# Linear attention rounds of a two-block model: heads innermost on TensorE, one masked copy per level over four score banks, the second exponents between two rounds, and no clearing of the score tile

## The reference, cut to what matters

```python
def step(state, inp):
    qc, kc, vc, gc = inp
    g = jnp.cumsum(gc, axis=2)
    seg = jnp.exp(jnp.where(tri[:, :, None], g[:, :, :, None, :] - g[:, :, None, :, :], -jnp.inf))
    att = jnp.sum(qc[:, :, :, None, :] * kc[:, :, None, :, :] * seg, axis=-1)
    o = (jnp.einsum('bhij,bhjv->bhiv', att, vc)
         + jnp.einsum('bhid,bhdv->bhiv', qc * jnp.exp(g), state))
```

## Time and profile before

| What | Value |
|---|---|
| median of 3 runs | 2586.05 us (2585.83 to 2586.1) |
| profiled execution, first to last instruction (its span) | 2580.6 us |
| the profiled execution's own time | not listed apart from its span; the median is 5.45 us above the span |
| mean granted TensorE clock | 0.968 of full speed |
| TensorE matmul busy | 2439.7 us (95%) |
| VectorE busy | 1693.0 us (66%) |
| ScalarE busy | 1374.6 us (53%) |
| GpSimd busy | 410.1 us (16%) |

### The profile page before, as it was taken

The page is one execution under the profiler, slowest core; times in us unless marked ns, Lnnn a source line. Parts: engine busy times, 40 slices in busy tenths (PEclk is TensorE's granted clock), DMA queues, the critical chain, the costliest instruction groups (busy, mean ns, idle before and its releaser), DMA issues.

```text
span 2580.6 us, 32016 instructions
## 1 busy us (share of the span) xinstructions
PE 2439.7 (95%) x11845; PEld 1981.6 (77%) x11845; DVE 1693.0 (66%) x2386; ACT 1374.6 (53%) x1737; POOL 410.1 (16%) x225
## 2 busy tenths in 40 slices
PE   7999899989988899999999999979989988998998
PEld 6987688888766687787787787868768877776886
DVE  4846565467564689898898898854555555355554
ACT  4543254445432578787787787735434434543443
POOL 2155000002540000000000000046510005550000
PEclk9998899989998899999999999989999998999999
DMA  7434375435331899999999999853465525346550
GB/s 222 169 109 147 100 260 195 133 100 186 130 132 34 289 346 366 331 341 353 331 357 336 331 364 329 284 161 129 170 225 202 183 89 170 128 150 212 196 196 33
DMA packets 381701, 549.38 MB, mean 213 GB/s; under 512 B 27221, under 2 KB 283593, under 8 KB 381465
## 3 DMA queue, kind: packets, MB, share of 16 engines
q1 hardware_dynamic: 377392, 535.82, 61.1%
q0 software_dynamic: 3920, 11.58, 1.7%
q10 hardware_dynamic: 288, 0.59, 0.1%
HBM read 546.91 MB, written 1.05 MB: 212 GB/s over the span
## 4 chain that ended last, share of the span: by engine, by line
PE 64%; DVE 3%; DMA 1%; ACT 1%; issue 1%; POOL 0%; DVEq 0%; ACTq 0%
PE mb L904 13%; PE mb L906 12%; PE mb L905 12%; PE pb L904 5%; PE pb L905 5%; PE pb L906 5%; PE pb L1349 2%; PE mb L1259 1%; PE pb L1299 1%; PE pb L887 1%; PE mb L1275 1%; DMA ring<-in_w_in 1%; PE mb L1385 0%; PE pb L1335 0%; PE pb L1334 0%
## 5 line engine op out<-in xcount | busy, mean ns | idle before, releaser
L2540 DVE TENSOR_TENSOR w_lo<-ring,w_hi 128x1024 fp32r<-128x1024 f32 x444 | 533.4, 1223 | 210.0 <-ACT w_hi L1645 184.2
L904 PE MATMUL mb<-w_hi,hT_hi 128*128 128x512 f32 x1232 | 493.5, 401 | 2.9 <-DVE w_lo L2540 2.6
L1645 ACT ACTIVATE w_hi<-ring 128x1024 fp32r<-128x1024 f32 x340 | 347.9, 1053 | 269.5 <-DMA ring<-in_w_in 101.9
L906 PE MATMUL mb<-w_lo,hT_hi 128*128 128x512 f32 x1232 | 481.0, 390 | 0.0
L756 POOL TENSOR_TENSOR w_lo<-ring,w_hi 128x1024 fp32r<-128x1024 f32 x152 | 373.3, 2484 | 457.1 <-ACT w_hi L1645 456.9
L904 PE MATMUL pb<-w_hi,hT_hi 128*128 128x512 f32 (+1 forms) x928 | 357.1, 385 | 10.2 <-DVE low_rows L2540 5.7
L2540 DVE TENSOR_TENSOR w_lo<-down_w,w_hi 128x1024 fp32r<-128x1024 f32 x242 | 293.6, 1223 | 87.6 <-ACT w_hi L1645 79.3
L905 PE MATMUL pb<-w_hi,low_rows 128*128 128x512 f32 (+1 forms) x928 | 347.6, 375 | 0.0
L906 PE MATMUL pb<-w_lo,hT_hi 128*128 128x512 f32 (+1 forms) x928 | 347.0, 374 | 0.0
L1794 ACT ACTIVATE w_hi<-ring 128x1024 fp32r<-128x1024 f32 x256 | 267.0, 1056 | 19.9 <-PE mb L906 13.0
L905 PE MATMUL mb<-w_hi,xg_lo 128*128 128x512 f32 x704 | 274.6, 390 | 0.0
(11 more groups left out here) (454 smaller groups left out, 3778.1 us busy)
## 6 DMA issues: line engine op xcount, KB each, us to landing
ring<-in_moe_w SPq DMA_DIRECT2D x128, 1024.0 KB, 7.9
ring<-in_w_in SPq DMA_DIRECT2D x50, 2048.0 KB, 8.1
down_w<-in_moe_w SPq DMA_DIRECT2D x88, 1024.0 KB, 11.3
third_gu<-in_moe_w SPq DMA_DIRECT2D x48, 1024.0 KB, 9.6
down_w<-in_w_ffn_down SPq DMA_DIRECT2D x22, 1024.0 KB, 10.0
ring<-in_w_out SPq DMA_DIRECT2D x8, 2048.0 KB, 8.0
ring<-in_ffn_w SPq DMA_DIRECT2D x16, 1024.0 KB, 7.9
ring<-in_w_ffn_gate SPq DMA_DIRECT2D x16, 1024.0 KB, 5.4
```

The source lines that it names most:

```text
L904: mm(o, a_hi, hi, start=start, stop=False)
L906: return mm(o, a_hi, lo, start=False, stop=stop)
L1645: f(w_hi[:, m % NPIECE], src, ACT.Copy).then_inc(w_hi_ready, 1)
L2540: return tt(dst, src, hi.bitcast(F32), ALU.subtract)
```

## The change

Five edits. (1) The four banks mb0 to mb3 are declared as one PSUM tensor of four banks, so that one instruction can read all four. (2) A helper `score_pairs` takes the heads of the retention and of the mLSTM in pairs: the wide product of both, then the narrow product of both. (3) In the rounds of the gated linear attention the loop over heads becomes the innermost. (4) `gla_put_levels` copies each level with one `copy_predicated` over all four banks (two per round in place of eight), and the last round with one copy in place of four; the clearing of probs is gone. (5) `gla_levels` is cut in two: `gla_exponents` and `gla_factors`; the second exponents are now made between the copies of round 0 and round 1, the second factors stay behind the copies of round 1, and the wait for round 1's products stands just ahead of the factors.

```diff
--- before.py
+++ after.py
@@ -416,7 +416,8 @@
         lat_s, lat_m, lat_r = small[:, 120:126], small[:, 126:130], small[:, 130:134]
 
         pb = [ctx.enter_context(nc.psum_tensor(f"pb{n}", [P, 512], F32)) for n in range(4)]
-        mb = [ctx.enter_context(nc.psum_tensor(f"mb{n}", [P, 512], F32)) for n in range(4)]
+        mb_all = ctx.enter_context(nc.psum_tensor("mb", [P, 4, 512], F32))
+        mb = [mb_all[:, n] for n in range(4)]
 
 
         filled, act_emptied, dve_emptied = sem("pb_filled"), sem("pb_act_emptied"), sem("pb_dve_emptied")
@@ -1030,6 +1031,19 @@
                 mm(bank[:, 0:S], kT[:, 0:P], qT, start=True, stop=True)
                 return mm(bank[:, S:S + P], kT[:, P:S], qT[:, P:S], start=True, stop=True)
 
+            def score_pairs(kT, qT):
+
+
+                for a in (0, 2):
+                    rows_of = lambda h: slice(64 * (h % 2), 64 * (h % 2) + 64)
+                    for h in (a, a + 1):
+                        r = rows_of(h)
+                        mm(mb[h][:, 0:S], kT[r, h // 2, 0:P], qT[r, h // 2, :], start=True, stop=True)
+                    for h in (a, a + 1):
+                        r = rows_of(h)
+                        ins = mm(mb[h][:, S:S + P], kT[r, h // 2, P:S], qT[r, h // 2, P:S], start=True, stop=True)
+                return ins
+
             def weigh_values(banks, v, w=64):
                 for i in range(T):
                     for h in range(NH):
@@ -1105,10 +1119,7 @@
                 gate(L, 1, 0, 1)
                 pe.wait_ge(ml_arg, 4 * (L + 1))
                 pe.wait_ge(conv_ready, 2 * L + 2)
-                for h in range(NH):
-                    r = 64 * (h % 2)
-                    ins = score_head(mb[h], conv[r:r + 64, 8 + h // 2, :], conv[r:r + 64, 6 + h // 2, :])
-                ins.then_inc(scores_mm, 1)
+                score_pairs(conv[:, 8:10], conv[:, 6:8]).then_inc(scores_mm, 1)
                 gate(L, 1, 1, 0)
                 pe.wait_ge(probs_ready, 3 * L + 2)
                 weigh_values(mb[0:2], lambda j, h: u_ml[:, j, h * (ML_V + 1):(h + 1) * (ML_V + 1)], ML_V + 1)
@@ -1124,10 +1135,7 @@
                 merge(L, 0)
                 pe.wait_ge(qkt_ready, L + 1)
                 pe.wait_ge(o_read, 4 * L + 2)
-                for h in range(NH):
-                    r = 64 * (h % 2)
-                    ins = score_head(mb[h], ret_qk[r:r + 64, 2 + h // 2, :], ret_qk[r:r + 64, h // 2, :])
-                ins.then_inc(scores_mm, 1)
+                score_pairs(ret_qk[:, 2:4], ret_qk[:, 0:2]).then_inc(scores_mm, 1)
                 gate(L, 2, 0, 0)
                 gate(L, 2, 0, 1)
                 pe.wait_ge(probs_ready, 3 * L + 3)
@@ -1143,20 +1151,17 @@
                         pe.wait_ge(gla_kq, 2 * L + rnd // 2 + 1)
                     if rnd:
                         pe.wait_ge(gla_put, 5 * L + rnd)
-                    for h in range(NH):
-                        r = slice(32 * h, 32 * h + 32)
-                        if rnd < 4:
-                            for s_ in range(2):
-                                lev = 2 * rnd + s_
-                                for i in range(T):
-                                    t_ = slice(i * P, (i + 1) * P)
-                                    kk, qq = (gla_k[r, lev % 4, t_], gla_q[r, lev % 4, t_]) if lev < 7 else (
-                                        ch_in[r, 11, t_], ch_in[r, 10, t_])
-                                    ins = mm(mb[h][:, s_ * S + i * P:s_ * S + (i + 1) * P], kk, qq, start=True, stop=True,
-                                             tile_position=(32 * h, 0))
-                        else:
-                            ins = mm(mb[h][:, 0:P], gla_k[r, 3, 0:P], gla_q[r, 3, P:S], start=True, stop=True,
-                                     tile_position=(32 * h, 0))
+                    for n in range(2 * T if rnd < 4 else 1):
+                        lev, t_ = 2 * rnd + n // T, slice(n % T * P, (n % T + 1) * P)
+                        for h in range(NH):
+                            r = slice(32 * h, 32 * h + 32)
+                            if rnd == 4:
+                                kk, qq = gla_k[r, 3, 0:P], gla_q[r, 3, P:S]
+                            elif lev < 7:
+                                kk, qq = gla_k[r, lev % 4, t_], gla_q[r, lev % 4, t_]
+                            else:
+                                kk, qq = ch_in[r, 11, t_], ch_in[r, 10, t_]
+                            ins = mm(mb[h][:, n * P:(n + 1) * P], kk, qq, start=True, stop=True, tile_position=(32 * h, 0))
                     ins.then_inc(gla_mm, 1)
                     if rnd < 2:
                         gate(L, 3, 0, rnd)
@@ -2113,11 +2118,9 @@
                             else:
                                 link(ins)
 
-            def gla_levels(L, half):
-
-
-                if half:
-                    v.wait_ge(gla_mm, 5 * L + 2)
+            def gla_exponents(L, half):
+
+
                 for n in range(4):
                     b = 1 << (4 * half + n)
                     g = gT[:].rearrange("p (m s b) -> p m s b", s=2, b=b)
@@ -2126,23 +2129,27 @@
                     tt(e[:, :, 0], ref, g[:, :, 0], ALU.subtract)
                     ins = tt(e[:, :, 1], g[:, :, 1], ref, ALU.subtract)
                 ins.then_inc(gla_arg, 1)
+
+            def gla_factors(L, half):
+
                 v.wait_ge(gla_exp, 2 * L + half + 1)
+                if half:
+                    v.wait_ge(gla_mm, 5 * L + 2)
                 tt(gla_k, gla_e, ch_in[:, 11:12].to_broadcast([P, 4, S]), ALU.mult)
                 tt(gla_q, gla_e, ch_in[:, 10:11].to_broadcast([P, 4, S]), ALU.mult).then_inc(gla_kq, 1)
 
             def gla_put_levels(L, rnd):
 
                 v.wait_ge(gla_mm, 5 * L + rnd + 1)
-                for h in range(NH):
-                    if rnd == 4:
-                        ins = cp(probs[:, h, P:S], mb[h][:, 0:P])
-                        continue
-                    dst = probs[:, h, :].rearrange("p (a i) -> p a i", i=P)[:, 0:3:2, :]
+                if rnd == 4:
+                    ins = cp(probs[:, :, P:S], mb_all[:, :, 0:P])
+                else:
+                    dst = probs[:].rearrange("p h (a i) -> p h a i", i=P)[:, :, 0:3:2, :]
                     for s_ in range(2):
-                        src = mb[h][:, s_ * S:(s_ + 1) * S].rearrange("p (a i) -> p a i", i=P)
-                        msk = levmask[:, 2 * rnd + s_].bitcast(U32).unsqueeze(1).to_broadcast([P, T, P])
+                        src = mb_all[:, :, s_ * S:(s_ + 1) * S].rearrange("p h (a i) -> p h a i", i=P)
+                        msk = levmask[:, 2 * rnd + s_].bitcast(U32).unsqueeze(1).unsqueeze(1).to_broadcast([P, NH, T, P])
                         ins = nc.vector.copy_predicated(dst, msk, src)
-                        if not (h == NH - 1 and s_ == 1):
+                        if s_ == 0:
                             link(ins)
                 ins.then_inc(gla_put, 1)
                 v.wait_ge(gla_put, 5 * L + rnd + 1)
@@ -2279,7 +2286,8 @@
                     tt(probs[:, h, 0:S], mb[h][:, 0:S], retdecay[:, h, 0:S], ALU.mult)
                     ins = tt(probs[:, h, S:384], mb[h][:, S:384], retdecay[:, h, 0:P], ALU.mult)
                 ins.then_inc(probs_ready, 1)
-                gla_levels(L, 0)
+                gla_exponents(L, 0)
+                gla_factors(L, 0)
                 take_y(L, 2)
                 for i in range(T):
                     ins = cp(y[:, i], mb[i][:, 0:MW])
@@ -2289,10 +2297,10 @@
                 merge(L, 1)
 
                 v.wait_ge(pv_mm, 4 * L + 3)
-                link(nc.vector.memset(probs[:].rearrange("p h n -> p (h n)"), 0.0))
                 gla_put_levels(L, 0)
+                gla_exponents(L, 1)
                 gla_put_levels(L, 1)
-                gla_levels(L, 1)
+                gla_factors(L, 1)
                 gla_put_levels(L, 2)
                 merge(L, 2, (0,))
                 gla_put_levels(L, 3)
```

## The result

The changed kernel takes 2566.48 us (median of 4 runs, 2562.36 to 2568.26) against 2586.07 us before (4 runs): a ratio of 0.9932, 95% interval 0.9914 to 0.995. That is 19.6 us faster, 3.5 us above the predicted 2563 and inside the range.

What follows compares the result with a forecast made beforehand. Bound: a chain hopping between TensorE and VectorE from round 0 to the weighing. Gains 13.1 (layer 0) + 10.7 (layer 1) + 0.4 (score pairs) - 1.0 (clock) = 23.2 us, so 2586.05 becomes 2563 us; range 2556 to 2573.

Steps and rivals of the forecast that it cites:

- rival (a): Before round 2, GpSimd goes first and both second factors wait: 2.2 us more per layer, 2567.5 us; chance 0.22.
- my own case: First factor ahead of GpSimd, second waits for one low part, round 2 at 242.75: 2563 us; chance 0.40.
- Rounds 1.10 us: On TensorE, heads innermost bring round start to next gate from 2.75 to 1.10 us, saving 1.65 per round.
- rival (c): New head order does nothing, or a wide masked copy costs four narrow ones: 2571 us; chance 0.18.
- Masked copy 1.26 us: On VectorE, a masked copy of 1024 elements takes 1260 ns, two in a chain some 2.55 us.
- Round 1 and exponents: In layer 0, round 1 starts at 233.9 in place of 236.55; the moved exponents end at X = 235.65.
- Both arrive at X + 2.6: First factor and GpSimd's low part due together after the exponents' end X; second factor done at about X + 7.1.
- 14.3 us from round 2 to the weighing: VectorE's chain there takes 14.3 us in place of 20.27 in layer 0 and 18.80 in layer 1.
- 1.0 on merge sums beside GpSimd: Two sums in the merge's first half meet GpSimd's last low parts, losing 1.0 us in all (bounds 0 and 2.7).
- 0.5 us per layer for the clock behind the weighing: Lower clock behind the weighing left as it is but for a 0.5 us loss per layer.
- The sum: Weighing earlier by 13.1 us in layer 0 and 10.7 in layer 1; with 0.4 and -1.0, 23.2 us in all.
- Score pairs 0.1 us each: Pairing the heads' score products wins 0.1 us at each of four places, 0.4 us (bounds 0 and 1.3).

Runs made afterwards that it cites:

- E10: Changed kernel plus one idle 128x256 copy on ScalarE ahead of the transposed y, so GpSimd starts a little later: 2562.43 us, ratio 0.9924.
- E4: Changed kernel with ScalarE making the first two high parts after the sigmoid of gate 3,0, releasing GpSimd's work later: 2558.73 us, ratio 0.9899.
- E7: Changed kernel with the second factors ahead of copies 1, right behind the exponential: 2557.11 us, ratio 0.9897.
- E11: Changed kernel with the heads outermost again in the rounds: 2566.23 us, ratio 0.9937.
- E6: Changed kernel with the second exponents moved back behind copies 1: 2566.01 us, ratio 0.9925.
- E9: The changed kernel run again, unaltered: 2565.5 us, ratio 0.9934.
- E8: E4's kernel with half of gate 3,1,0 ahead of round 4 and half ahead of the weighing, filling TensorE's waits: 2545.07 us, ratio 0.9842.
- E12: E7's kernel with half of gate 3,1,0 ahead of round 4 and half ahead of the weighing: 2540.47 us, ratio 0.9834.

## Why the prediction was right, and where it was not

The direction, the size and the range held. The order of events that I gave the highest chance did not: **rival (a) happened**, GpSimd ahead and both factors waiting, and its 2567.5 us is 1.0 us from the measured time. Its chance of 0.22 beside 0.40 for my own case did not fit what I called a tie. Step by step:

- *Rounds 1.10 us*: right to the hundredth (226.68 to 227.78), and rival (c)'s first half, that the order is immaterial, falls with it.
- *Masked copy 1.26 us*: too low, 1.316. Between 256 and 1024 elements it grows by (1316 - 447) / 768 = 1.13 ns per element, not by the 1.06 of the plain copy whose slope I borrowed.
- *Round 1 and exponents*: forecast 7.8 us behind round 0, measured 7.60; the exponents end at X = 235.97, 9.29 us behind round 0, forecast 9.55.
- ***"Both arrive at X + 2.6 ... the order is a dead heat, and this is the middle"***: the step that failed. GpSimd came at X + 2.60 as worked out, VectorE at X + 2.65: the copies were 0.15 us longer per pair than I took (2.70, not 2.55), more than the 0.05 us by which GpSimd won. Both factors then waited, the second was done at X + 9.4 and not X + 7.1: 2.3 us per layer, against the 2.2 that I had put on it. E10 turned the tie and got 2.2 us per layer back up to round 2, and 1.9 and 2.1 in the stage; E4 and E7 show by two routes that the factors' length was GpSimd's doing. I had the price right. What I called the middle was the time with VectorE ahead, taken because it lies between no collision and GpSimd ahead; but two estimates whose difference is smaller than their error leave one of two values, and which one is open.
- *14.3 us from round 2 to the weighing*: measured 14.2 and 14.3, but by luck, from other terms. I put 1.0 on merge sums beside GpSimd; they took 0.69 each, because GpSimd was through by 249.88. Instead round 2 took 2.09 us and not 1.17 at the lower clock, after a wait of 4.26 us.
- *0.5 us per layer for the clock behind the weighing*: from the weighing to the transposes 18.15 and 18.41 us now, 17.79 and 17.73 before: 1.0 us in both layers together, as taken.
- *The sum*: stage gains of 13.1 + 10.7 - 1.0 = 22.8 us forecast, 18.7 measured. The difference, 4.1 us, is the tie in two layers, 2 x 2.2 us, but for 0.3.
- *Score pairs 0.1 us each*: 1.61 to 1.50, right for the group read; the mLSTM's, which I didn't read, wins nothing in layer 0.

What the prediction didn't see is that its parts stand in for one another. It credits each round with 1.65 us and the move with bringing the factors forward; E11 and E6 take away either and lose nothing that these runs can tell. Each part alone gained 0.17 to 0.26%, and all together 0.68%, not the 0.91% of the four ratios added; their intervals alone don't settle that difference, and E11, beside E9 in one group, is the clearest evidence. It shows two reasons: the shorter rounds bring VectorE's factors 2.6 us earlier, onto one more of GpSimd's low parts, and where TensorE is made faster while another engine sets the pace, the time goes to waits, and the clock then falls. E6 shows a third: exponents brought forward bring GpSimd forward too. Not tried alone: the score pairs, and the copies with the clearing gone but neither order nor move.

## What to carry to other kernels

When a step is moved, follow what it releases on the other engines, and if two of them are then due on a shared resource within the error of the estimate, don't take the middle: forecast both cases, and look for an order in which instructions that don't meet there (here copies out of PSUM) lie beside the other engine's work. When TensorE's own work is shortened in a stage that another engine paces, put independent products into the waits in the same edit: here that alone was worth 0.57% of the time before (E8 against E4) and 0.63% (E12 against E7), some 15 us and about as much as the whole change. Together with the order of E7 it makes 25 us over the changed kernel (E12 against E9).

## What the runs showed of the hardware that was not expected

VectorE and GpSimd took turns instruction by instruction when both had a queue of instructions reading two SBUF operands: 1.22 us became 3.44 and 3.37, and low parts of 2.4 us became 3.33. The prediction had these turns in its working. The Trainium skill, SBUF — State Buffer, Who interferes with whom, says that a VectorE instruction with two SBUF inputs contends with a GpSimd instruction that reads SBUF, and, of VectorE's two-port modes, that whoever issues first has the shared ports for its whole instruction: the ends of the rows show the same here for two SBUF inputs, for each instruction by itself. What was not expected is how little decides it: an offset of 0.03 to 0.05 us settled which of the two went first, the same one in all four stages traced of this kernel (two layers, two traces).
